# Three f32r passes on split operands in the output stage, and the delta output norms moved one stage later

## What is computed

```python
o_a = hgrn2_mixer(a_q, a_f, a_i, a_g, lower_bounds[l], hgrn_norm_g[l])
o_b = gla_mixer(b_q, b_k, b_v, b_code, b_g, ...)
o_c = mla_mixer(c_q, c_kv, c_kr, ...)
o_d = gdn_mixer(d_q, d_k, d_v, d_beta, d_a, d_z, ...)   # ends: rms_norm(o, norm_g) * silu(z)
mix = jnp.concatenate([o_a, o_b, o_c, o_d], axis=-1).astype(h.dtype) @ w_out[l]
x = x + rms_norm(mix, post_mix_g[l])
```

## Time and profile before

| | |
|---|---|
| median of 3 runs | 2296.11 us (2295.84 to 2297.59) |
| profiled execution: time, span | 2292.07 us, 2290.3 us |
| busy: TensorE, weight load | 95%, 68% |
| busy: VectorE, ScalarE, GpSimd | 53%, 39%, 2% |
| mean granted TensorE clock | 0.980 |
| DMA | 159.79 MB, mean 70 GB/s |
| load of one ring slot (1 MB), issue to landing | 4.7 us median |
| span at which stages of layer 0 start | first gated 192.8, second gated 237.1, output 402.0, feed-forward 421.3 |
| the same of layer 1 | first gated 978.2, second gated 1022.5, output 1187.4, feed-forward 1206.8 |

### The profile page before, as it was taken

How to read it: one execution, slowest core, us unless ns; L and a number is a source line. 1 busy time by engine, 2 the same in 40 slices (tenths; PEclk the granted TensorE clock), 3 DMA queues, 4 the chain that set the end, 5 groups by cost and what they waited for, 6 DMA issues and landing times. The chain is left out here.

```text
span 2290.3 us, 35396 instructions
## 1 busy us (share of the span) xinstructions
PE 2169.8 (95%) x14540; PEld 1555.1 (68%) x14540; DVE 1208.1 (53%) x2075; ACT 898.2 (39%) x1611; POOL 45.6 (2%) x36
## 2 busy tenths in 40 slices
PE   7999999899999999989998999998999988999998
PEld 5784454588888777744446888886877566887546
DVE  5553344676662285543546666524537774444554
ACT  5423234433333354233344333333346553323462
POOL 2000001000000020000010000000000000000000
PEclk9999999999999999999999999999999999999999
DMA  5201110122222221011112222222221102222001
GB/s 199 74 3 46 48 55 32 63 92 97 106 92 92 92 74 56 22 38 56 38 38 80 104 92 92 102 82 97 97 90 56 38 19 92 93 92 85 26 1 37
DMA packets 23920, 159.79 MB, mean 70 GB/s; under 512 B 3024, under 2 KB 3664, under 8 KB 4944
## 3 DMA queue, kind: packets, MB, share of 16 engines
q1 hardware_dynamic: 23760, 157.53, 19.3%
HBM read 155.43 MB, written 2.10 MB: 69 GB/s over the span
## 5 line engine op out<-in xcount | busy, mean ns | idle before, releaser
L673 DVE TENSOR_TENSOR arena_r<-ring,arena_r 128x512 fp32r<-128x512 f32 x448 | 313.1, 706 | 453.7 <-ACT arena_r L664 450.9
L664 ACT ACTIVATE arena_r<-ring 128x512 fp32r<-128x512 f32 x448 | 278.3, 629 | 597.8 <-PE banks L714 566.4
L712 PE MATMUL banks<-oT_r,arena_r 128*128 128x512 f32 x1104 | 449.5, 407 | 13.0 <-DVE arena_r L673 9.0
L714 PE MATMUL banks<-oT_r,arena_r 128*128 128x512 f32 x1104 | 432.4, 392 | 0.0
L713 PE MATMUL banks<-hT_r,arena_r 128*128 128x512 f32 x928 | 363.6, 392 | 0.0
L713 PE MATMUL banks<-arena_r,arena_r 128*128 128x512 f32 x704 | 276.3, 392 | 0.0
L712 PEld LDWEIGHTS banks<-oT_r,arena_r 128*128 128x128 f32 x1104 | 208.8, 189 | 71.4 <-DVE arena_r L944 11.8
L712 PE MATMUL banks<-arena_r,arena_r 128*128 128x512 f32 x592 | 240.3, 406 | 15.2 <-DVE arena_r L704 10.9
L714 PEld LDWEIGHTS banks<-oT_r,arena_r 128*128 128x128 f32 x1104 | 208.5, 189 | 44.5
L714 PE MATMUL banks<-arena_r,arena_r 128*128 128x512 f32 x592 | 232.6, 393 | 0.0
L713 PEld LDWEIGHTS banks<-hT_r,arena_r 128*128 128x128 f32 x928 | 175.8, 189 | 41.6 <-issue 7.2
(11 more groups left out here) (387 smaller groups left out, 2927.7 us busy)
## 6 DMA issues: line engine op xcount, KB each, us to landing
ring<-weights SPq DMA_DIRECT2D x142, 1024.0 KB, 4.7
xT<-x_features SPq DMA_DIRECT2D x2, 1024.0 KB, 6.2
arena<-memory SPq DMA_DIRECT2D x2, 1024.0 KB, 4.9
y_features<-xT SPq DMA_DIRECT2D x8, 256.0 KB, 2.0
const<-constants SPq DMA_DIRECT2D x1, 1088.0 KB, 15.7
const<-constants SPq DMA_DIRECT2D x1, 512.0 KB, 16.4
arena<-positions SPq DMA_DIRECT2D x1, 256.0 KB, 2.7
small<-small_vectors SPq DMA_DIRECT2D x2, 68.5 KB, 6.4
```

The costliest lines, as they stand in the source:

```text
L664: act.activation(hi, self.stream.block(b, n), ACT.Copy).then_inc(self.chip.sem("hi_ready"), 1)
L673: vec.tensor_tensor(lo[:, 0:n * P], self.stream.block(b, n), hi[:, 0:n * P].bitcast(F32), ALU.subtract).then_inc(self.chip.sem("lo_ready"), 1)
L712: pe.matmul(out, w_hi, hi, start=k == 0, stop=False)
L714: ins = pe.matmul(out, w_lo, hi, start=False, stop=k == nk - 1)
```

## The change

It has two parts.

In `out_stage` the first two units stay f32. The other six (twelve products) become split products: the two feature tiles are split at the stage's start into `parts`, the 12 blocks of weights in three chunks of four, all with tiles of their own. ScalarE's and VectorE's lists begin with that splitting (VectorE splits the third chunk after its first add). SyncE's one load of the stage waits for the third chunk and for the two f32 units, where it waited for the eighth unit. `whole` is the count of units ahead of the split ones.

The norms of the delta outputs leave `delta_stage`: its two `blk64` matmuls, its table load, its two Ln and two Exp and its two last products. The squares and the gated outputs go to other tiles (`DZS`, `DZ`), which nobody uses before they are read again. The same operations come into `gla_stage` when `group == 0` (`left = 2`): the matmuls after the two projection blocks behind L1681, Ln and Exp ahead of the stage's own squares, the products ahead of the stage's own.

```diff
     def loads(self, sp, u0, u1, split=None, ahead=0, whole=0):
...
                     sp.wait_ge(self.chip.sem("lo_ready"), split.last_chunk(i - RING) + 1)
+                    if whole:
+                        sp.wait_ge(self.chip.sem("dense_ready"), whole)
...
 def delta_stage(chip, stream):
...
-            meanwhile.tensor(pe, blocks=4)
-            pe.wait_ge(chip.sem("sq_ready"), 2)
-            for h in range(2):
-                made(pe.matmul(fill(f"out{h}"), chip.c("blk64"), SQ[h], start=True, stop=True))
             meanwhile.tensor(pe)
...
-            act.preload_act_table_set(EXP_LN)
-            for h in range(2):
-                rstd_of(f"out{h}", RN[h], 64.0)
             meanwhile.scalar(act)
...
-            for h in range(2):
-                vec.wait_ge(chip.sem("rstd_ready"), 5 + h)
-                v(tt(chip.o(6 + h), OG[h], RN[h], ALU.mult))
...
 def gla_stage(chip, stream, group, names, evac, work):
...
+    left = 2 if group == 0 else 0
+    NORM = DELTA + left
+    D_SQ, D_OUT, D_R = ([chip.t(b + h) for h in range(left)] for b in (DZS, DZ, 11))
...
                 meanwhile.tensor(pe, blocks=2 if hgrn else 1)
+                for h in range(left):
+                    pe.matmul(chip.T.fill(pe), chip.c("blk64"), D_SQ[h], start=True, stop=True).then_inc(chip.sem("t_ready"), 1)
                 pe.wait_ge(chip.sem("cut_ready"), j + 1)
...
             meanwhile.scalar(act, 2 if hgrn else 3)
+            for h in range(left):
+                act.activation(D_R[h], chip.T.full(act, DELTA + h), ACT.Ln, bias=chip.c("eps"), scale=1.0 / 64.0).then_inc(chip.sem("t_used"), 1)
+                act.wait_ge(chip.sem("t_used"), DELTA + h + 1)
+                act.activation(D_R[h], D_R[h], ACT.Exp, scale=-0.5).then_inc(chip.sem("rstd_ready"), 1)
...
+            for h in range(left):
+                vec.wait_ge(chip.sem("rstd_ready"), h + 1)
+                v(tt(chip.o(6 + h), D_OUT[h], D_R[h], ALU.mult))
...
 def out_stage(chip, stream):
...
+    whole = 2
+    parts = lambda k: (chip.t_r(20 + k), chip.t_r(22 + k))
+    split = Split(chip, stream, u0 + whole, u1, [(chip.t_r(24 + 2 * i), chip.t_r(25 + 2 * i)) for i in range(4)], whole=whole)
...
-            stream.loads(sp, u0, u1)
+            stream.loads(sp, u0, u1, split, whole=whole)
...
-            for k in range(KD):
-                product(chip, pe, stream, u0 + k, lambda k: chip.o(4 + k))
+            for u in range(u0, u0 + whole):
+                product(chip, pe, stream, u, lambda k: chip.o(4 + k))
+            for u in range(u0 + whole, u1):
+                split_product(chip, pe, split, u, parts,
+                              each=(lambda k: pe.wait_ge(chip.sem("x_lo"), k + 1)) if u == u0 + whole else None)
...
+            for k in range(2):
+                hi_part(chip, act, k, chip.o(4 + k), parts(k)[0])
+            split.scalar_chunks(act, len(split.chunks))
...
+            for k in range(2):
+                lo_part(chip, vec, k, chip.o(4 + k), *parts(k))
+            split.vector_chunks(vec, 2)
             for k in range(KD):
+                if k == 1:
+                    split.vector_chunks(vec, len(split.chunks))
                 v(vec.tensor_tensor(chip.h(k), chip.h(k), chip.dense.take(vec), ALU.add), chip.sem("dense_used"))
```

More of the change, by code:

```diff
@@ L577, in next_loads, with loads @@
             sp.wait_ge(self.chip.w_loaded[b], 16 * (self.loaded + loads + 1))
-    def loads(self, sp, u0, u1, split=None, ahead=0):
+    def loads(self, sp, u0, u1, split=None, ahead=0, whole=0):
         for i in range(RING, self.plan.slots):
@@ L602, with __init__ @@
 class Split:
-    def __init__(self, chip, stream, u0, u1, tiles, group=0, head=()):
+    def __init__(self, chip, stream, u0, u1, tiles, group=0, head=(), whole=0):
         self.chip, self.stream, self.tiles, self.head = chip, stream, tiles, head
@@ L624, in __init__ @@
             if units[last][1] + units[last][2] == b + n:
-                self.used.append((last, "dense_ready", last - u0 + 1))
+                self.used.append((last, "dense_ready", whole + last - u0 + 1))
             else:
@@ L1099, in delta_stage @@
     U, W, WT, PT, R, STATE, VN = NT, N16T, N16, C32, N8, N4T, N4
-    RN, SQ, OG = [chip.t(5), chip.t(6), *X16], LT, N
+    RN = [chip.t(5), chip.t(6), *X16]
     TINY = chip.t(55)
@@ L1383, in _ @@
                 act.wait_ge(chip.sem("o_ready"), zz + 1)
-                act.activation(by_tokens(pair_view(39))[:, zz], ring.full(act, at[f"o{zz}"]).rearrange("p (t h c) -> p t h c", t=TT, h=2),
+                act.activation(by_tokens(pair_view(DZS))[:, zz], ring.full(act, at[f"o{zz}"]).rearrange("p (t h c) -> p t h c", t=TT, h=2),
                                ACT.Square).then_inc(chip.sem("sq_ready"), 1)
-            act.preload_act_table_set(EXP_LN)
-            for h in range(2):
-                rstd_of(f"out{h}", RN[h], 64.0)
             meanwhile.scalar(act)
@@ L1518, in _ @@
                 bank, done = take(f"o{zz}")
-                tt(by_tokens(pair_view(35))[:, zz], bank.rearrange("p (t h c) -> p t h c", t=TT, h=2),
+                tt(by_tokens(pair_view(DZ))[:, zz], bank.rearrange("p (t h c) -> p t h c", t=TT, h=2),
                    by_tokens(pair_view(DZ))[:, zz], ALU.mult).then_inc(done, 1)
@@ L1564, in gla_stage @@
     E_EARLY, KDT, E_LATE, UPD = nj + 1, nj + 5, nj + 6, nj + 10
-    NORM = UPD + 2
+    DELTA = UPD + 2
+    left = 2 if group == 0 else 0
+    NORM = DELTA + left
+    D_SQ, D_OUT, D_R = ([chip.t(b + h) for h in range(left)] for b in (DZS, DZ, 11))
     GRAMS = 4
@@ L1829, in _ @@
             for j in range(nj):
-                vec.wait_ge(chip.sem("rstd_ready"), j + 1)
+                vec.wait_ge(chip.sem("rstd_ready"), left + j + 1)
                 v(tt(chip.o(out + j), OG[j], R[j], ALU.mult))
```

## The result

The changed kernel takes 2280.97 us (median of 4 runs, 2278.86 to 2283.80), against 2296.85 us for the kernel before beside it; the ratio is 0.9930, 95% interval 0.9913 to 0.9948. The forecast was 2284.8 us with a range from 2281.8, so the kernel is 0.8 us faster than the range allowed, and the gain is 15.9 us where 11.3 were forecast. The profiled execution has a span of 2279.4 us, where 2279.0 was forecast.

A forecast was written before the change was run, and what follows sets the result against it. The prediction took TensorE, busy 95% of the span, as the bound. Two layers x (4.35 us from delta and first gated stages + 1.3 from the output stage) = 11.3 us, off the 2296.11 median: 2284.8 us, range 2281.8 to 2289.0.

The forecast's parts named there:

- What ends the delta tail: Delta stage's end: last Sigmoid, then barrier, with no table load between the Sigmoids; gated stage starts 4.76 us sooner.
- The clock right behind it: First gated stage's start: with idleness ahead cut from 3.98 to 0.95 us, full clock returns, gaining 1.69 us a layer.
- The norms' price in the gated stage: First gated stage: two f32 matmuls coming in cost 1.72 us a layer, plus a stall of 0.38 us.
- The output stage, in its steps: Output stage: later first add, two-bank wait, then VectorE's 1.44 us a unit as bound; 1.3 us sooner a layer.
- the 0.1 us for the restart: Output stage: allowance for TensorE's restart at 405.75 after its bank wait, added in timing the third add at 407.5.
- The load issued earlier: Output stage: SyncE's only load, 1 MB, is issued some 9 us earlier; costed at nothing.
- Rival (c): Output stage: TensorE stands between units and drops to 1.2 GHz; 5.4 us a layer slower, 2307 us; chance 0.03.
- the clock term: First gated stage only: the low clock behind the delta gap vanishes, gaining the whole 1.69 us in each layer.
- Rival (e): More gain: TensorE paces the output stage, or feed-forward's low stretch goes too; 2282 to 2283.5 us; chance 0.08.
- the starting point: Whole kernel: the gain is subtracted from the median of three runs, 2296.11 us, 4.0 us above the profiled execution.
- The stall of 0.38 us: First gated stage: Square ready at about 234.2, TensorE wants it at 233.86; ends nothing and 1.0 us.

The follow-up runs named there:

- gap_filled: Kernel before plus four dummy f32 matmuls of constants in TensorE's idle gap at the delta stage's end, nothing moved: 2288.79 us against 2295.61, ratio 0.9970.
- out_only: Kernel before with only the split products of the output stage, old delta and gated stages kept: 2292.32 us against 2294.93, ratio 0.9988.
- delta_only: Kernel before with only the delta output norms moved into the first gated stage, old output stage kept: 2281.67 us, ratio 0.9941.
- one_fill: Changed kernel plus one dummy f32 matmul of constants at the second gated stage's end: 2280.97 us, ratio to the kernel before 0.9945.

## Why the prediction was wrong

**Right.** What ends the delta tail (the Sigmoid, then the barrier), that no table is loaded, and 4.56 us for 4.76. The clock right behind it: 1.69 us, and `gap_filled` shows the idleness as its cause. The norms' price in the gated stage: it is 44.35 us with them and 42.60 without them at full clock (`gap_filled`), 1.75 for the 2.1 forecast; the two matmuls are 1.72. The output stage, in its steps: first add, third, last, pitch, bound, 1.27 us for 1.3, and `out_only` 2.6 us for 2.6. No run shows the 0.1 us for the restart in that working by itself; the third add came 1.80 us after the third unit's start, where 0.1 + 1.38 + 0.27 were added. The load issued earlier costs nothing that any trace shows. Rival (c) did not happen as told, as the clock is 1.00 while the units run, but a smaller thing near it did: the low stretch over the stage's end, in 2 of the 6 output stages traced of the changed kernel, which costs 0.5 to 0.6 us there. That the forecast span (2279.0) and the first traced one (2279.4) agree is luck: the touched stages gave 10.3 us and the untouched ones 0.6.

**The step that failed: the clock term.** It is the step that takes "the whole 1.69 us as gained" and stops there. It counts the low stretch in the stage behind the gap, found in rows 2 and 4, and puts the change of the clock in the rest of the kernel at nothing, without a reason. But closing that gap is worth more than the stage behind it shows. The clock term measured 6.0 us (give or take 1.7) in place of 3.4, by the mean clock over 79 and 14 executions, and `gap_filled`, where it stands alone, gave 6.9 (4.8 to 9.2); `delta_only` puts the surplus with the moved norms. One place that the prediction did not read is the third gated stage, untouched, which in the kernel before started at 1.2 GHz in both layers: a window there shows 0.67. Rival (e) named this sort of thing, at the feed-forward stage only, and with a chance of 0.08; its 2282 is still above the measured 2280.97. By which way a gap in the delta stage acts on stages two and more behind it stays open.

**A term mis-sized: the starting point.** The prediction subtracts from 2296.11 us, the median of three executions. Seventy-nine have a median of 2295.3 and reach from 2288.6 to 2299.2; four of the changed kernel gave 2280.97 where fourteen give 2281.3. The range had no width for this draw. From 2295.3 the forecast would have been 2284.0, so of the 3.8 us between forecast and measurement 0.8 is the start. Less the 2.6 us by which the clock term was short, the sum is 2281.4. That is bookkeeping and no test, as the 2.6 come from the same executions.

**The stall of 0.38 us** is not there (its own terms, 234.18 less 233.86, give 0.32). The kernel before, with the blocks that correspond to those at 224.75 after the change:

```profile
230.75 1.98 PE L748 MATMUL banks<-hT,ring 128*128 128x512 f32 x4
...
232.57 1.02 PE L1696 MATMUL banks<-arena,const 128*128 128x512 f32 x2
```

The norm's matmul starts 1.82 us behind these blocks' start both before (230.75 to 232.57) and after (224.75 to 226.57). Its weights, loaded 1.39 us behind it before (232.14), are loaded at 226.49 after, 0.35 us late, for they wait for the Square; the matmul starts on time all the same. The wait ate the lead that the weight load has on its matmul. The prediction took a late weight load for a late matmul.

**Open.** What decides whether an idle piece of 1.4 us is followed by a low stretch. The same code ahead of the third gated stage had it in some executions and not in others. The two parts alone gave 13.3 and 2.6 us, 15.9 together, and the whole change 13.2. By means the difference is 3.4 us with a standard error of 1.3, more than scatter easily makes; the low stretches at the end of the new output stage are a candidate, and no run shows that they are the reason.

## What to carry to other kernels

Where the clock falls behind an idle piece, its price is not only in the stage behind it: list all low stretches of the trace, untouched stages included, before taking them as fixed, and leave them in the range. A span that comes out as forecast proves little when stages that nobody touched move by several us: compare stage by stage, over more than one trace. A few dummy matmuls in a gap cost nothing here, where the engine stood still anyway, and they measure what the idleness costs before anything is rebuilt. When a product gets cheaper on TensorE, count what the evacuating engine has per unit: here 1.44 us against 1.38 decided what was left of the gain.

## What the runs showed of the hardware

Four f32 matmuls of constants in a 4 us gap made the kernel 6.9 us faster (4.8 to 9.2). Through that gap the granted clock stayed at 1.00; it was 0.64 over the 4.8 us after TensorE had started again. Executions of one and the same program spread over 10 us, and over 20 in `one_fill`, with the granted clock; an attention stage is 57.6, 59.3, 60.9, 62.5 or 64.2 us, in steps of about 1.65, at a granted clock from 1.00 down to 0.89. The output stage of the changed kernel is 18.13 us, or 18.7 with a low stretch at its end. Adding 3.4 us of work to the kernel before cost 2.5 (0 to 4.8), and the same to the changed one 6.8 by means (4.1 to 9.5). One weight load was held up by 0.35 us and its matmul still started on time.
